# Input projection as three split products, Silu in one ScalarE pass, state transfers moved to SyncE's queue

## The reference, cut to what matters

```python
proj = u @ w_in                       # u: 264 rows x 1024; w_in: 1024 x about 9,500 columns
z, xbc, dt_raw, q, k, v, gate_a, gate_b = jnp.split(proj, cuts, axis=-1)
xbc_c = jax.nn.silu(causal_dwconv(xbc_ext, conv_w, conv_b))
y, h_new = ssd_scan(xs, dt, A, Bm, Cm, h0)
y = (y + d_skip[:, None] * xs).reshape(Bsz, T, D_INNER) * jax.nn.silu(z)
branch_a = group_rms_norm(y, ssm_norm_g) @ w_out_ssm     # mean of squares over 512 channels
# attention with three dilations -> branch_b; merge by sigmoid gates; @ w_out; layer norm
# then top-4-of-32 experts: 32 x (1024x2048 and 1024x1024) weights; layer norm
```

## Time and profile before

| | us |
|---|---|
| median of 3 runs | 1509.5 (1508.16 to 1512.73) |
| the profiled execution, its own time | 1509.7 |
| its span in the trace | 1508.0 |
| TensorE busy | 1390.3 (92%) |
| VectorE busy | 502.9 (33%) |
| ScalarE busy | 222.0 (15%) |
| GpSimd busy | 168.6 (11%) |
| moved by DMA | 539.18 MB, mean 358 GB/s |

### The profile page before, as it was taken

One profiled execution on the slowest core, in us unless ns is written; L12 is line 12 of the kernel. 1 busy time (PEld: TensorE's weight loads), 2 busy tenths in 40 slices (PEclk: granted clock), 3 DMA queues, 4 the chain that ended last, 5 costly groups with the idle time before them and its releaser, 6 DMA issues.

```text
span 1508.0 us, 24345 instructions
## 1 busy us (share of the span) xinstructions
PE 1390.3 (92%) x9768; PEld 675.6 (45%) x9768; DVE 502.9 (33%) x824; ACT 222.0 (15%) x536; POOL 168.6 (11%) x223
## 2 busy tenths in 40 slices
PE   5999999999899889999999899989998999899984
PEld 4887888887576433333322232223222322232221
DVE  0454556585545432222211222122112221222124
ACT  1334222241430100000000000000000000000002
POOL 0022445500110000000000000000000000000002
PEclk9999999999899889999999999999999999999998
DMA  8697999864868989999999999999999999999993
GB/s 244 204 338 262 300 346 338 285 231 141 278 238 299 357 299 418 420 416 417 419 418 416 417 419 418 416 418 418 418 417 417 418 419 416 417 419 418 416 416 121
DMA packets 164649, 539.18 MB, mean 358 GB/s; under 512 B 11036, under 2 KB 90236, under 8 KB 130996
## 3 DMA queue, kind: packets, MB, share of 16 engines
q1 hardware_dynamic: 123712, 502.59, 84.4%
q10 hardware_dynamic: 39748, 31.88, 7.2%
q0 software_dynamic: 1152, 4.20, 0.8%
HBM read 522.39 MB, written 60.43 MB: 386 GB/s over the span
## 4 chain that ended last, share of the span: by engine, by line
PE 45%; SPq 27%; DMA 22%; DVE 3%; issue 2%; ACT 0%; POOL 0%; ACTq 0%; DVEq 0%; POOLq 0%
PE psum L1578 17%; DMA wmx<-in_w_down_dram 16%; SPq L425 16%; SPq L421 10%; PE psum L1981 6%; PE psum L1996 5%; DMA wmh<-in_w_down_dram 3%; PE psum L1748 3%; PE psum L1889 2%; PE psum L1969 2%; DMA keys<-in_cache_kv_w_dram 1%; PE psum L2015 1%; DMA gn_rows<-in_ssm_norm_g_dram 1%; PE psum L1656 1%; PE psum L1652 1%
## 5 line engine op out<-in xcount | busy, mean ns | idle before, releaser
L1578 PE MATMUL psum<-xT,wraw 128*128 128x264 f32 x1184 | 274.7, 391 | 0.5 <-ACT xT L635 0.5
L1981 PE MATMUL psum<-wnat,xst 128*32 128x512 f32 x2480 | 272.5, 594 | 0.4 <-DVE xst L1457 0.4
L1578 PEld LDWEIGHTS psum<-xT,wraw 128*128 128x128 f32 x1184 | 226.4, 193 | 43.2 <-issue 4.9
L1491 DVE STREAM_TRANSPOSE hturn<-psum 128x1024 f32<-128x1024 f32 x32 | 40.0, 1250 | 404.6 <-PE psum L1981 404.6
L1981 PEld LDWEIGHTS psum<-wnat,xst 128*32 128x32 f32 x2480 | 77.6, 110 | 172.5 <-issue 172.5
L1996 PE MATMUL psum<-wmx,hst 128*64 128x512 f32 x496 | 118.8, 603 | 31.9 <-DMA wmx<-in_w_down_dram 31.9
L1996 PE MATMUL psum<-wmh,hst 128*64 128x512 f32 x496 | 119.0, 602 | 29.6 <-DMA wmh<-in_w_down_dram 29.6
L1981 PE MATMUL psum<-wmh,xst 128*32 128x512 f32 x1056 | 119.2, 592 | 0.0
L582 POOL COPY gcol<-gm 128x3 f32 (+1 forms) x32 | 17.0, 532 | 849.4 <-DVE hb L1494 848.4
L979 ACT ACTIVATE sg<-hb 128x512 f32<-128x512 f32 x32 | 20.2, 630 | 526.6 <-DVE hb L1499 526.6
L1969 PE MATMUL psum<-x,oneh 128*32 128x256 f32 x1584 | 94.2, 387 | 3.1 <-DVE oneh L1441 3.1
(11 more groups left out here) (377 smaller groups left out, 1201.8 us busy)
## 6 DMA issues: line engine op xcount, KB each, us to landing
wnat<-in_w_gate_up_dram SPq DMA_DIRECT2D x155, 1024.0 KB, 20.3
wmh<-in_w_gate_up_dram SPq DMA_DIRECT2D x66, 1024.0 KB, 24.2
wmh<-in_w_down_dram SPq DMA_DIRECT2D x62, 1024.0 KB, 26.2
wmx<-in_w_down_dram SPq DMA_DIRECT2D x62, 1024.0 KB, 23.4
wraw<-in_w_in_dram SPq DMA_DIRECT2D x37, 1024.0 KB, 10.5
whm<-in_w_gate_up_dram SPq DMA_DIRECT2D x33, 1024.0 KB, 22.4
out_dram<-in_cache_kv_w_dram SPq DMA_DIRECT2D x32, 1023.5 KB, 6.7
out_dram<-hs ACTq DMA_DIRECT2D x8, 1024.0 KB, 12.0
```

The source lines that it names most:

```text
L1491: v.transpose(hturn[:, :], psum[:, 0:2, :].rearrange("p h c -> p (h c)")).then_inc(S("hidden_out"), 1)
L1578: last = mm(bank[6 + m % 2][:, 0:T], w[:, k, :], xT[:, k, :], start=(k == 0), stop=(k == KT - 1))
L1981: last = mm(bank[h][q * QW:(q + 1) * QW, :], xst[:, h, k, :], w[:, q, :, :, :], start=(k == 0), stop=(k == GU_CH - 1))
```

## The change

- The projection's operands are split in two: a high part as float32r, and the rest, which is the value less its high part. A tile is now high x high, high x rest (of x) and rest (of w) x high: 24 float32r matmuls in place of 8 float32 ones. `xh` and `xl` replace `xT`.
- The high part of a weight tile is an ACT copy of 128x1024 (`high(m)`, into a ring of 4, `wh`), four tiles ahead; the rest is a DVE subtraction of 128x1024 (`low(m)`, in place, `wlow`).
- `RING` is 5 slots where it was 7. A slot's load must have landed when ACT makes the high part.
- z is evicted through Silu, and the convolution ends in Silu on ACT. The separate sigmoids, POOL's multiplication (L507) and DVE's product with `zsig` (L1172) go.
- `state_in`, `state_back` and `decay_in` move from ACT's queue to SP's, between the weight loads.
- POOL adds four squares to one, so TensorE's sums take 4 matmuls where they took 16.
- SP loads no weights until the parameter rows and the tokens have landed.
- Units 33 to 36 and the first scores are placed a little differently on TensorE, and the first loads of the output weights come one unit later or more.

The diff, cut:

```diff
-RING = 7
-NRING = 5
+RING = 5
+HL = 4
...
+            sp.wait_ge(S("rows_in"), 80)
+            sp.wait_ge(S("x_in"), 32)
             for u in range(N_PROJ):
                 if u >= RING:
                     sp.wait_ge(S("tile_done"), 2 * (u - RING) + 2)
-                    if u != 8:
+                    if u > 7:
                         move_cache(next(pieces))
                 load(u, wraw[:, u % RING, :].rearrange("p (k n) -> p k n", k=KT), w_in_v[:, :, w_in_col(u):w_in_col(u) + 256])
+                if u == 9:
+                    sp.wait_ge(S("a_out"), 16)
+                if u in (9, 11, 13):
+                    decay_in((u - 9) // 2)
+                elif u >= 19 and u % 2 and u < 13 + 4 * GROUPS:
+                    decay_in((u - 13) // 2)
+                if u in (10, 14):
+                    state_in((u - 10) // 4)
+                elif u >= 20 and u % 2 == 0 and u < 18 + 4 * GROUPS:
+                    state_back((u - 20) // 2)
+                elif u >= 21 and u % 2 and u < 19 + 2 * (TS - 1):
+                    state_in((u - 17) // 2)
+                elif u == 34:
+                    state_back(TS - 1)
...
-            for u in range(XT // 2):
-                pool.wait_ge(S("csig_done"), u + 1)
-                pool.wait_ge(S("tail_psum"), u + 1)
-                g.tensor_tensor(xbc[:, 2 * u:2 * u + 2, :], ctmp[:, u % 3, :, :], csig[:, u % 2, :, :],
-                                ALU.mult).then_inc(S("conv_done"), 1)
...
+            for gi in range(GROUPS):
+                pool.wait_ge(S("ysq_ready"), gi + 1)
+                sq = ysq[:, gi % 2, :, :]
+                own.then(g.tensor_tensor(sq[:, 0:2, :], sq[:, 0:2, :], sq[:, 2:4, :], ALU.add))
+                g.tensor_tensor(sq[:, 0, :], sq[:, 0, :], sq[:, 1, :], ALU.add).then_inc(S("ysq_sum"), 1)
...
+            def high(m):
+
+                raw_ready(act, m // 2)
+                if m >= HL:
+                    act.wait_ge(S("tile_done"), m - HL + 1)
+                a.activation(high_of(m), half_of(wraw, m), ACT.Copy).then_inc(S("high_done"), 1)
...
-                    a.activation(zz[:, m - Z_AT, :], out, ACT.Copy).then_inc(S("bank_free"), 1)
+                    a.activation(zz[:, m - Z_AT, :], out, ACT.Silu).then_inc(S("bank_free"), 1)
...
+                if m + HL < NT:
+                    high(m + HL)
...
+            def low(m):
+
+                dve.wait_ge(S("high_done"), m + 1)
+                v.tensor_tensor(half_of(wlow, m), half_of(wraw, m), high_of(m).bitcast(F32), ALU.subtract).then_inc(
+                    S("low_done"), 1)
...
             def project(m):
 
-                if m % 2 == 0:
-                    raw_ready(pe, m // 2)
+                pe.wait_ge(S("low_done"), m + 1)
                 if m >= 2:
                     pe.wait_ge(S("bank_free"), m - 1)
-                w = half_of(m)
+                out = bank[6 + m % 2][:, 0:T]
+                hi, lo = high_of(m), half_of(wlow, m)
                 for k in range(KT):
-                    last = mm(bank[6 + m % 2][:, 0:T], w[:, k, :], xT[:, k, :], start=(k == 0), stop=(k == KT - 1))
+                    mm(out, hi[:, k, :], xh[:, k, :], start=(k == 0), stop=False)
+                    mm(out, hi[:, k, :], xl[:, k, :], start=False, stop=False)
+                    last = mm(out, lo[:, k, :], xh[:, k, :], start=False, stop=(k == KT - 1))
                 last.then_inc(S("tile_done"), 1)
...
+                pe.wait_ge(S("ysq_sum"), gi + 1)
+                mm(bank[gi][:, 0:T], ones[:, :], ysq[:, gi % 2, 0, :], start=True, stop=True).then_inc(S("ss_psum"), 1)
```

More of the change, by code:

```diff
@@ L397, in native @@
                 sp.dma_start(dst, src).then_inc(S(f"native_landed{native_slot(i)}"), 16)
-            for i in range(NRING):
+            for i in range(RING):
                 native(i)
@@ L858, in _ @@
                          ACT.Copy).then_inc(S("qkvs_ready"), 1)
-            for m in range(68, NT):
-                slot(m)
+            slot(72)
+            slot(73)
             def cached(gi, kv):
@@ L1037, in _ @@
                                    op1=ALU.min).then_inc(stage("dt_abs"), 1)
+            low(4)
+            low(5)
             dve.wait_ge(S("params_ready"), 4)
@@ L1077, in convolve @@
                 v.tensor_tensor(t, t, stsum[:, f:f + 2, :], ALU.add).then_inc(S("ctmp_done"), 1)
-            for u in range(XT // 2):
-                convolve(u)
+            for u in range(1, XT // 2):
+                convolve(u - 1)
+                low(2 * u + 4)
+                low(2 * u + 5)
+            convolve(11)
+            low(28)
+            low(29)
             dve.wait_ge(S("dtok_ready"), 3)
@@ L1176, in _ @@
                     last.then_inc(S("yz_ready"), 1)
+            for m in range(66, 69):
+                low(m)
             for gi in range(GROUPS):
@@ L1788, in query_spread @@
                 mm(bank[at + 1][:, 0:256], one, q[:, 512:768], start=True, stop=True).then_inc(S("q_psum"), 1)
-            scores(0)
-            scores(1)
-            unit(35)
-            scores(2)
-            scores(3)
             unit(36)
+            for h in range(4):
+                scores(h)
             for n in range(4):
```

185 lines of the change are left out of this document (100 added, 85 removed).

## The result

The changed kernel takes 1498.4 us (median of 5 runs, 1497.3 to 1502.0), the kernel before, in 5 runs beside it, 1509.5: ratio 0.9925, interval 0.9908 to 0.9943. It is faster by 11 us; the prediction said 40, and its range ended at 1497. The profiled execution took 1498.7 us, its span 1497.0.

What follows compares the result with a forecast made beforehand. TensorE was taken to bound the projection ahead of the experts' stream, with VectorE and GpSimd next in the rounds. Terms -26 + 0.4 - 23 + 5.5 + 3 = -40 on 1509.7 gave 1469.7, forecast 1470 us, range 1450 to 1497.

Steps and rivals of the forecast that it cites:

- A: The forecast itself: VectorE and GpSimd hold the round at 20 to 22.5 us; 1455 to 1485 us, chance 0.45.
- a first round of 14 us and six of 21: Round stage: VectorE's short first round, then six at 21 us with waits for GpSimd; the stage gives nothing.
- The sign that I had named: In the rounds, TensorE idle before projection tiles, waiting for VectorE's `wlow`, some 5 us a round.
- Start, -5.6: Kernel start: rows land after about 8 us with weights held back; first tile at 21.8 us, not 27.4.
- The product, 112.5 ns: Projection on TensorE: a float32r product costs a quarter of a float32 matmul; a tile takes 2.70 us, 0.90 less.
- rival D: Projection: a float32r product costs more than about 152 ns, making the kernel slower; about 1628 us at 225 ns; chance 0.09.
- the 3 us for waits of loads: Convolution stage: 3 us added for waits, with 82 us of DMA work and a ring of 5.
- First round product 8.5 us behind the stage: Start of the rounds: VectorE's first round product comes 8.5 us after the convolution stage, not 12.8.
- Tail, 62: Last round product to last tile: VectorE's path takes 62 us, TensorE's 61.4, in place of 85.1; -23 us.
- Heads, 32: Attention: the first gates product comes 32 us behind the last tile, where it was 26.3; +5.5 us.
- Rival B: Rounds: subtractions fall between GpSimd's instructions and DMA sets the round at 18.5 us; 1451 us, chance 0.17.
- Rival C: Rounds: SP's in-order waits for state and landed writes hold up loads, a round takes 24 us; 1496 us, chance 0.22.

Runs made afterwards that it cites:

- x1: The changed kernel without VectorE's 74 subtractions, the third product repeating the high part of w (rest of w left out): 1471.8 us, ratio 0.9758 to the kernel before.
- x2: The changed kernel with GpSimd's two state passes on one sixteenth of each state, the rest of the update left out: 1483.1 us, ratio 0.9832.
- x8: The changed kernel with GpSimd's two passes over a state each cut into four instructions, nothing left out: 1492.0 us, ratio 0.9895.
- x9: The changed kernel with masks and last subtractions in the tail's idle time, and GpSimd's state passes in quarters: 1484.7 us, ratio 0.9839.
- x5: The changed kernel without SyncE's two waits ahead of the weights, so weights load beside parameter rows and tokens: 1499.1 us, ratio 0.9940.
- x11: The changed kernel with VectorE's first round product ahead of the subtractions for tiles 30 and 31: 1493.3 us, ratio 0.9900.
- x14: x9 with VectorE's first round product also ahead of the two subtractions for tiles 30 and 31: 1486.5 us, ratio 0.9835.
- x12: x1 also without the 18 cache copy pieces that SyncE issues between the loads of units 16 to 33: 1468.4 us, ratio 0.9740.
- x7: The changed kernel with decay rows and state transfers issued from ScalarE's queue again, at the old places: 1498.8 us, ratio 0.9939.
- x3: The changed kernel with two of three masks and the subtractions of tiles 69 to 71 moved into VectorE's idle time in the tail: 1493.7 us, ratio 0.9909.

## Why the prediction was wrong, and where it was right

The mechanism of A was right: TensorE's gain in the rounds turned into waits for VectorE, whose subtractions themselves wait for GpSimd, and x1 and x2 each remove it. Its size, 139.0 us from first to last product where 140 was forecast, is partly luck. The forecast had a first round of 14 us and six of 21; measured were 22.2 and a mean of 19.5, and the two errors cancel. In the first round VectorE waited 5.3 us for a high part and one subtraction took 5.62, which the 14 us left out. The sign that I had named, TensorE waiting for `wlow` some 5 us a round, did not show: it idled 2.5 us a round, for VectorE's `hT` and `acb` and for ScalarE. The Trainium skill (SBUF — State Buffer, Who interferes with whom) has VectorE's wait for GpSimd as an exclusive lock for a whole instruction; x2's flat line (1.28 us at most) and x8's subtractions, 2.32 us at most beside the pieces, agree. The same section says that copy, cast and tensor_scalar can contend when they run in a two-port mode; x9's cast of 1.34 us against 0.36 agrees with that.

What failed are terms around it, each by its row:

- *Start, -5.6.* The step that put the rows' landing at 8 us, 2 MB at the stretches' rate, failed twice. It left out the 3.35 us before the last row's transfer is issued, and that transfer takes 9.9 us with no weights beside it. 3.35 + 9.9 is 13.25, nearly all of the 5.4 us of the miss. Holding the weights back moves the rows by only 3.5 us (x5) or 2.5 (against before). A small transfer's time was priced by bytes.
- *The product, 112.5 ns.* Right in kind, rival D is out; it measured 121. That is 0.20 us a tile, 5.2 us in the convolution stage and 3.6 in the tail. In the convolution stage the first 23 products at 220 ns add 2.3 and the stretch of half clock 1.3; the 3 us for waits of loads that I had added did not occur (TensorE 88.07 of 88.07 us busy) and offset a part. The rest, some 3 us the other way, is not traced.
- *First round product 8.5 us behind the stage.* The forecast took 4.3 us off the 12.8 of before with no row for it, and that is 3.9 of the 6.4 us: with no subtractions at all (x1) the product comes 12.4 us behind the stage, with the product put first (x11) 12.3. ScalarE's decay factors and VectorE's decay product come ahead of it and ended 9.9 us behind the stage already before the change, and TensorE has only two tiles in that stretch, 1.8 us to gain at the forecast's price. The other 2.5 us are the subtractions: I did not follow the high part for tile 30 through ScalarE's order, where it stands behind two loads of 1.28 us and the decay factors, and VectorE's order passes the wait on. By x11 and x14, taking these back is worth nothing that can be measured at the end.
- *Tail, 62.* VectorE's path and TensorE's own 61.4 were nearly alike in the sum, and I took the longer one as if the two ran beside each other without meeting. TensorE was busy for 64.9 us, which is the 61.4 and the product's 3.6; the other 8.3 us it sat idle, 3.1 for GpSimd's sums, 2.6 for VectorE's `hT` and 2.6 for a subtraction. The path through ScalarE's squares, GpSimd's sums and TensorE's queue costs VectorE 10.4 us of waits where I had 4 us. With no subtractions and no cache copies beside it (x12) the tail is 65.3 us, TensorE's own length; x1 alone, at 71.0, cannot show that, since its weights came late.
- *Heads, 32.* The norm ended 8 us ahead of the last tile (334.1 to 342.4), not 4; but two subtractions and 8.7 us of masks stand between the norm and the first head, which began at 345.6, 3.2 us behind the last tile, and the first gates product came 35.9 us behind it.

Rival B's floor was wrong: with the port free a round takes 17.8 us (x2), and without the subtractions TensorE sets it at 17.7 (x12). Rival C's mechanism did not show: with the transfers on the other queue the kernel is no faster (x7), and between the first and last round product VectorE waited for a high part three times, 7.1 us in all. The measured time is still C's, 1496, by another road: misses of one sign.

"Faster" held, by 11 us and not by 40. That the misses had one sign has in part a cause too: at the first round product, in the tail and at the heads, 21.5 us together less 3.6 for the product's price, I let an engine start as soon as its input was there, or took its path for shorter than its rows; but the engines run in a written order.

Open: what x3 is worth by itself, why x9 gained more than x3 and x8 add up to, whether GpSimd's sums cost anything, what made the 3.1 us behind the gates product, and what decides on the half clock in the convolution stage.

## What to carry to other kernels

When work is moved from the bounding engine to its neighbours, price the neighbours' order and not their idle share: a product that gets 0.7 us a tile cheaper here brought 9 to 11 us in 1500, because VectorE, idle for 43% of the round stage before, became the engine that the rounds waited for. Here, beside a long GpSimd instruction, a VectorE instruction with two SBUF inputs could last as long as that one and itself (5.62 us beside an addition of 4.6); cutting GpSimd's instructions costs it time and shortens the worst wait. And a forecast needs, for each engine that takes new work, its rows in the written order at the two ends of the stretch, where the new work stands first in line. And when an experiment takes one limit away, look for the next one before reading what is left: x1's tail is held up by late weights that the changed kernel does not wait for.
